# Values stationary, two query halves in two column tiles: turning the weighing of a float32 attention round

## What is computed

```python
h = rms_norm(x, g_pre) * (1 + scale) + shift
z = h @ w_in                     # q, k, v of A and B; q, k, v, gates of C; u
# A: 8 query heads, 2 kv heads, dim 64: softmax(q k^T / 8) @ v
# B: 4 heads, q and k in halves of 32, value dim 64
a = softmax(s1) - lam * softmax(s2);  o_b = rms_norm(a @ v, b_out_gain) * (1 - lam_init)
# C: bidirectional gated linear attention (GLA), then rms_norm per head
mixed = concat(o_a, o_b, o_c) * silu(u)
x_new = x + gate * rms_norm(mixed @ w_out, g_post)
```

## Time and profile before

| | before |
|---|---|
| median of three runs, us | 2540.59 |
| profiled execution: span, us | 2538.9 |
| profiled execution: own time beside the span | not recorded apart; the median lies 1.7 above the span |
| PE busy, share of the span | 2343.5, 92% |
| DVE, ACT, POOL busy, us | 1248.2, 874.2, 411.0 |
| attention of one layer, 563 to 1125 us: PE, DVE, ACT, POOL busy | 557.0, 267.2, 227.2, 82.9 of 562 |
| output block of one layer, 1125 to 1270 us: PE, DVE busy | 126.8, 80.4 of 145 |

### The profile page before, as it was taken

The page is one execution under the profiler, slowest core; times in us unless marked ns, Lnnn a source line. Parts: engine busy times, 40 slices in busy tenths (PEclk is TensorE's granted clock), DMA queues, the critical chain, the costliest instruction groups (busy, mean ns, idle before and its releaser), DMA issues. The chain is left out here.

```text
span 2538.9 us, 37284 instructions
## 1 busy us (share of the span) xinstructions
PE 2343.5 (92%) x14005; PEld 2004.6 (79%) x14005; DVE 1248.2 (49%) x2247; ACT 874.2 (34%) x1424; POOL 411.0 (16%) x344
## 2 busy tenths in 40 slices
PE   5799999879999999979958999998899999999798
PEld 3678987559999999977736789876599999999676
DVE  5667100865444454465466770008645444544554
ACT  5432211413444334442153322124143444344421
POOL 0211220420111111010002121114101111110200
PEclk9899999879999999989979999998799999999899
DMA  7332121010111111023273322210110111010232
GB/s 251 108 109 83 56 85 51 20 46 13 29 29 29 24 23 29 18 74 125 92 257 100 110 82 67 75 52 13 46 31 12 29 29 29 19 28 18 100 100 100
DMA packets 215017, 164.65 MB, mean 65 GB/s; under 512 B 162236, under 2 KB 164736, under 8 KB 214912
## 3 DMA queue, kind: packets, MB, share of 16 engines
q1 hardware_dynamic: 214912, 163.26, 21.4%
HBM read 124.80 MB, written 38.42 MB: 64 GB/s over the span
## 5 line engine op out<-in xcount | busy, mean ns | idle before, releaser
L1295 DVE TENSOR_REDUCE neg_max_parts<-work 128x1 f32<-128x512 f32 (+1 forms) x608 | 394.6, 687 | 410.6 <-PE work L1120 400.0
L1248 ACT ACTIVATE probs<-scores 128x1024 f32<-128x1024 f32 x320 | 327.7, 1025 | 566.7 <-PE scores L1138 338.1
L422 PE MATMUL z_acc<-w_hi,h_hi 128*128 128x512 f32 (+1 forms) x960 | 361.5, 377 | 12.4 <-DVE h_lo L539 7.6
L422 PE MATMUL z_acc<-w_hi,h_lo 128*128 128x512 f32 (+1 forms) x960 | 358.5, 373 | 0.0
L422 PE MATMUL z_acc<-w_lo,h_hi 128*128 128x512 f32 (+1 forms) x960 | 358.5, 373 | 0.0
L1159 PEld LDWEIGHTS att_out<-vB,probs 128*128 128x128 f32 x2688 | 336.4, 191 | 20.6 <-ACT probs L1248 7.7
L1159 PEld LDWEIGHTS att_out<-vA,probs 128*128 128x128 f32 x2688 | 339.3, 191 | 12.5
L1159 PE MATMUL att_out<-vB,probs 128*128 128x65 f32 x2688 | 336.2, 270 | 5.3 <-ACT probs L1248 4.8
L1159 PE MATMUL att_out<-vA,probs 128*128 128x65 f32 x2688 | 338.7, 270 | 0.0
L520 POOL TENSOR_TENSOR w_lo<-w_stage,w_hi 128x512 fp32r<-128x512 f32 (+1 forms) x112 | 134.7, 1231 | 824.1 <-ACT w_hi L455 824.1
L422 PEld LDWEIGHTS z_acc<-w_hi,h_hi 128*128 128x128 f32 x960 | 182.3, 190 | 47.4 <-DVE h_lo L539 9.2
(11 more groups left out here) (220 smaller groups left out, 3310.2 us busy)
## 6 DMA issues: line engine op xcount, KB each, us to landing
mod_w<-in_w_mod SPq DMA_DIRECT2D x24, 1024.0 KB, 7.6
w_stage<-in_w_in SPq DMA_DIRECT2D x96, 256.0 KB, 3.1
z_scratch<-z_out SPq DMA_DIRECT2D x60, 256.0 KB, 2.0
u_scratch<-z_out SPq DMA_DIRECT2D x40, 256.0 KB, 2.0
cv<-u_scratch SPq DMA_DIRECT2D x20, 512.0 KB, 5.8
out_y_sample<-y_tiles SPq DMA_DIRECT2D x16, 512.0 KB, 5.2
k_rawA<-z_scratch SPq DMA_DIRECT2D x16, 320.0 KB, 3.0
q_rawA<-z_scratch SPq DMA_DIRECT2D x16, 320.0 KB, 3.7
```

The lines of the kernel that those rows point to most:

```text
L422: mm = pe.matmul(acc, w_ap if w_first else h_ap, h_ap if w_first else w_ap, start=(k == 0 and q == 0), stop=(k == KD - 1 and q == 2))
L1248: act.activation(pr[:, b, :], sc[b][:, :, :].rearrange("p c n -> p (c n)"), ACT.Exp, scale=SCALE[u]).then_inc(s["a_exp"], 1)
L1295: dve.tensor_reduce(dst, src, AX_X, ALU.max, negate=True).then_inc(s["a_wkdve"], 1)
```

## The change

In the attention block the values become the stationary operand (64 columns) and the probabilities the moving one. The 1024 queries are two halves of 512; the first half's output stands on PSUM partitions 0 to 63, the second's on 64 to 127, so that they are two column tiles of the array. Outputs thus come transposed (head dimension on partitions) and stay so in `oa` and `ob`; the gate is made and stored transposed too, and the output block needs transposes for the GLA part alone. Row sums are no column of the values any more: GpSimd adds the probabilities of the key tiles (all but the last one in A, the last two in B) in `prob_sums`, and TensorE multiplies that sum and the left-out tiles by ones. The reciprocal is taken of 512 columns. `probs` has six buffers. The casts of the hi parts move from GpSimd to ScalarE. The steps stand in groups of two, the prompt is step 5 and no longer the last; all sixteen units are written out, without a loop. Two DMAs load B's gain by partition.

```diff
@@ attention: constants
-PREP_AT = (3, 3, 4, 4, 4, 3, 3, 3, 3, 0, 0)
-HALF = 5
+PROMPT_AT = 5
+TILE_AT = (0, 1, 2, 3, 4, None, 5, 6, 7, 8, 9)
+GROUPS = ((0, 1), (2, 3), (4, 5), (6, 7), (8, 9))
+NPB = 6
+DIRECT = {"A": 1, "B": 2}
@@ GpSimd
+            for p in range(UNITS):
+                u, h = of_unit(p)
+                for j in range(1, summed(p)):
+                    i = TILE_AT.index(j)
+                    n = p * STEPS + i
+                    pool.wait_ge(s["a_exp"], n + 1)
+                    a = acc[:, p % 2, :]
+                    if j == 1:
...
+                        ins = pool.tensor_tensor(a, pr[:, (n - 1) % NPB, :], pr[:, n % NPB, :], ALU.add)
+                    else:
+                        pool.wait_ge(s["a_add"], adds(p, i) - 1)
+                        ins = pool.tensor_tensor(a, a, pr[:, n % NPB, :], ALU.add)
+                    ins.then_inc(s["a_add"], 1)
+                    if j == 6 and p + 2 < UNITS:
+                        split_lo(pool, s, att, u, h + 1)
@@ TensorE
-                    mm = pe.matmul(o, probs, v[u][:, key, :], start=(j == 0 and t % HALF == 0),
-                                   stop=(j == KT_S - 1 or (j == KT_S and key == KT - 1)), skip_group_check=True)
+            def weigh(p, i):
...
+                pe.wait_ge(s["a_exp"], n + 1)
+                if i == 0:
+                    pe.wait_ge(s[f"a_v{u}"], 32 * (h + 1))
+                if i == 0 or i == PROMPT_AT:
+                    pe.wait_ge(s["a_out"], p + 1)
+                j = TILE_AT[i]
+                if j is not None:
+                    for rows, q in halves(NB):
+                        mm = pe.matmul(ob[rows, :], v[u][:, j, :], probs[:, q], start=(j == 0), stop=(j == KT_S - 1))
...
+            def sums(p):
+                u, h = of_unit(p)
+                pe.wait_ge(s["a_pout"], p + 1)
...
+                for x, src in enumerate(sources):
+                    if x == len(sources) - 1:
+                        pe.wait_ge(s["a_add"], adds(p, LAST))
+                    for rows, q in halves(NB):
+                        mm = pe.matmul(sm[rows, :], per["ones"][:, :], src[:, q], start=(x == 0), stop=(x == len(sources) - 1))
+                mm.then_inc(s["a_sum"], 1)
...
+            def run_unit(p):
+                nxt = p + 1
+                for g in range(len(GROUPS) - 1):
+                    pieces(nxt, 6 * g, 2)
+                    scores(p, GROUPS[g + 1][0])
+                    pieces(nxt, 6 * g + 2, 2)
+                    scores(p, GROUPS[g + 1][1])
+                    pieces(nxt, 6 * g + 4, 2)
+                    for i in GROUPS[g]:
+                        weigh(p, i)
+                pieces(nxt, 24, 2)
+                scores(p, LAST)
+                pieces(nxt, 26, 1)
+                for i in GROUPS[-1]:
+                    weigh(p, i)
+                pieces(nxt, PREP_LAST, PREP - PREP_LAST)
+                weigh(p, LAST)
+                sums(p)
+                if nxt < UNITS:
+                    for i in GROUPS[0]:
+                        scores(nxt, i)
@@ ScalarE, run_unit
+                for i in range(STEPS):
+                    exps(p, i)
+                    if nxt:
+                        if i in (1, 2, 3):
+                            for x in range(2 * i - 2, 2 * i):
+                                stand(nxt, x)
...
+                    if i == PROMPT_AT and p + 2 < UNITS:
+                        split_hi(u, h + 1)
@@ VectorE
+                    if p and i == 18:
+                        prompt_output(p - 1)
...
+            def prompt_output(p):
+                dve.wait_ge(s["a_pv"], p * STEPS + PROMPT_AT + 1)
+                dve.reciprocal(rsp[:, :], sm[:, P:2 * P]).then_inc(s["a_rs"], 1)
...
+            def output(p):
+                dve.wait_ge(s["a_sum"], p + 1)
+                dve.reciprocal(rs[:, :], sm[:, :]).then_inc(s["a_rs"], 1)
+                dve.wait_ge(s["a_rs"], 2 * p + 2)
+                weighted(p, ob, rs, 0, NB).then_inc(s["a_out"], 1)
...
-                do(dve.tensor_tensor(csq[:, :, :], oc[:, :, :], oc[:, :, :], ALU.mult))
+                for t in range(0, T, 2):
+                    do(dve.tensor_tensor(csq[:, :, :], oc[:, t:t + 2, :], oc[:, t:t + 2, :], ALU.mult))
...
@@ projection
-            if kind in ("z", "u"):
+            if kind == "z":
                 uses += [(b, kind, t) for t in range(T)]
+            elif kind == "u":
+                uses += [(b, f"u{m}", tb) for m in range(NB // P) for tb in range(3)]
@@ output block
-                dve.tensor_reduce(bst[:, t % 2, 0, :], bsq[:, :, :], AX_X, ALU.add).then_inc(s["o_bss"], 1)
+                do(dve.tensor_tensor(bd[:, t % 2, :, :], o[:, 0, :, tile_rows(t)], o[:, 1, :, tile_rows(t)], ALU.add))
+                dve.tensor_tensor(bsq[:, :, :], bd[:, t % 2, :, :], bd[:, t % 2, :, :], ALU.mult).then_inc(s["o_bsq"], 1)
...
+                do(dve.reciprocal(bst[:, b, :, :], bst[:, b, :, :]))
...
+                pe.matmul(bs[t % 2][:, :, :].rearrange("p k t -> p (k t)"), per["pair_ones"][:, :],
+                          bsq[:, :, :].rearrange("p k t -> p (k t)"), start=True, stop=True).then_inc(s["o_bss"], 1)
...
             turn(0)
+            turn(1)
+            turn(2)
```

More of the change, by code:

```diff
@@ L193, in _ @@
                 sp.dma_start(per["gains"][:, i, :], layer(io[name]).broadcast_to([P, HEAD_DIM])).then_inc(s["m_small"], 16)
+            for r in range(2):
+                sp.dma_start(per["b_gain"][r * B_V:(r + 1) * B_V, :], layer(io["b_out_gain"]).rearrange("a d -> d a")).then_inc(s["m_small"], 16)
             sp.dma_start(lam_c[:, :], layer(io["lam_consts"]).broadcast_to([P, 2])).then_inc(s["m_small"], 16)
@@ L398, in _ @@
                         store_z(b, t)
-                    elif kind == "u":
-                        store_u(b, t)
-            n = Z_BLOCKS * T + 2 * T
+                if kind == "u":
+                    for i in range(first_use[b], last_use[b] + 1):
+                        store_u(i)
+            n = Z_BLOCKS * T + len([u for u in uses if u[1][0] == "u"])
             for i in range(3):
@@ L1045, in attention_block, with of_unit, summed, adds @@
         m_cols = {A: qst2[:, :, HEAD_DIM:HEAD_DIM + 2], B: qst[B][:, :, 3 * B_QK:KR[B]]}
[L1046 to L1052, removed]
-            return 2 * h + (0 if u == A else 1)
+        def of_unit(p):
+            return "AB"[p % 2], p // 2
+        def summed(p):
+            return KT_S - DIRECT["AB"[p % 2]]
+        def adds(p, i):
+            before = sum(summed(x) - 1 for x in range(p))
+            j = len([t for t in TILE_AT[:i + 1] if t is not None and t < summed(p)])
+            return before + max(j - 1, 1)
+        def halves(t):
+            return [(slice(c * HEAD_DIM, (c + 1) * HEAD_DIM), slice(c * t, (c + 1) * t)) for c in range(2)]
         @block.sync
@@ new lines, in weigh @@
+            def weigh(p, i):
+                u, h = of_unit(p)
+                n = p * STEPS + i
+                probs = pr[:, n % NPB, :]
+                pe.wait_ge(s["a_exp"], n + 1)
+                if i == 0:
+                    pe.wait_ge(s[f"a_v{u}"], 32 * (h + 1))
+                if i == 0 or i == PROMPT_AT:
+                    pe.wait_ge(s["a_out"], p + 1)
+                j = TILE_AT[i]
+                if j is not None:
+                    for rows, q in halves(NB):
+                        mm = pe.matmul(ob[rows, :], v[u][:, j, :], probs[:, q], start=(j == 0), stop=(j == KT_S - 1))
+                else:
+                    for what in range(2):
+                        for c in range(2):
+                            for rows, q in halves(P):
+                                lhs = per["ones"][:, :] if what else v[u][:, KT_S + c, :]
+                                mm = pe.matmul(sm[rows, what * P:(what + 1) * P], lhs, probs[:, c * NB + q.start:c * NB + q.stop],
+                                               start=(c == 0), stop=(c == 1))
+                mm.then_inc(s["a_pv"], 1)
@@ new lines, in pieces @@
+            def pieces(p, first, n):
+                if p < UNITS:
+                    for i in range(first, first + n):
+                        prep(p, i)
+            def run_unit(p):
[19 more added lines that the diff above has]
+                        scores(nxt, i)
@@ new lines, in split_hi @@
+            def split_hi(u, h):
+                w = QK_W[u]
+                k, q, ks, qs = att["kraw"][u], att["qraw"][u], kst[u], qst[u]
+                act.wait_ge(s[f"a_raw{u}"], 48 * (h + 1))
+                if u == A:
+                    act.copy(ks[:, :, 0:w], k[:, :, :])
+                    act.copy(qs[:, :, w:2 * w], q[:, :, :])
+                else:
+                    for x in range(2):
+                        act.copy(ks[:, :, x * w:(x + 1) * w], k[:, :, :])
+                    act.copy(qs[:, :, 2 * w:3 * w], q[:, :, :])
+                act.copy(qs[:, :, 0:w], q[:, :, :]).then_inc(s[f"a_hi{u}"], 1)
```

384 lines of the change are left out of this document (176 added, 208 removed).

## The result

The changed kernel takes 2577.94 us (median, 2577.3 to 2578.28) against 2540.72 for the kernel before: ratio 1.0144, 95% interval 1.013 to 1.0159. It is 37 us slower; the forecast was 2529, 12 faster.

The account below looks back on a forecast made before the run. TensorE was taken as the bound, its weighing records paced by loads of the probabilities. Loop -12.6, first unit -4.4 and last unit +11 gave -6 a layer, -12 for two: 2540.6 - 12 = 2529 us, range 2455 to 2610.

Parts of the forecast that it names:

- rival (d): Attention loop: TensorE's clock spends 20 us a turn at half, +10 a pair, 2680 in total; chance 0.04.
- the first group of B: Start of a B unit, where pieces wait for ScalarE's casts between exponentials: 8.3 us against 5.3 dense.
- The pair's walk: Attention loop, step by step: A 33.2 plus B 36.3 make 69.5 us against 71.3, -12.6 a layer.
- the signs that the prediction named: Trace marks of a right forecast, such as a pair of 66 to 73 and B's cast waits of some 3 us.
- Column tiles: Weighing: products of the two 64-column tiles run together, so a key tile costs 0.86 us instead of 1.72.
- change of shape: TensorE's array form between pieces and weighings: a round trip costs 0.31 us, six a unit, 1.6.
- reciprocal: VectorE's reciprocal of the row sums, now 512 columns: 3.5 us, with two products 5.0 instead of 1.04.
- rival (c): Weighing: the column tiles run one after another for 512 columns, 2780 in total; chance 0.04.
- The first unit: First attention unit of a layer, from the last scores before it: 32.3 us instead of 36.7, -4.4 a layer.
- The last unit: Last attention unit, squares held by GpSimd's adds and output bare: 36.6 us against 25.7, +11 a layer.
- The output block: Output stage after attention, with fewer transposes and other VectorE work: together -3 to +4 us a layer.
- Rival (b): Unit ends: GpSimd's adds hold VectorE's small steps, 2 to 4 us a unit, 2600; with added handshakes chance 0.30.

Follow-up runs that it names:

- e1_fill: Changed kernel with four score products made twice more in the first group of every B unit but the last, filling TensorE's waits; 2552.47 us.
- e8: Changed kernel with each group's two weighings set apart between the pieces, from the second group on; 2594.11 us, ratio to before 1.0203.
- e5: Changed kernel with 16 of the 21 maxima in a unit reading only the first 256 columns of each bank; 2540.38 us, single run.
- e4: Changed kernel with GpSimd adding only the first pair of key tiles of each unit, so row sums lack tiles; 2561.56 us, single run.
- e2: Changed kernel with ScalarE's second casts of A's key pieces replaced by one later copy from SBUF; 2533.69 us, ratio to before 0.9967.
- e13: Changed kernel with both products of the first query half before both of the second, in four of five groups; 2577.66 us, single run.

## Why the prediction was wrong

**The step that failed** is rival (d), "The clock falls", at a chance of 0.04, and with it the first group of B, costed at the full clock though the text itself gave it "4.9 in 8.3". e1_fill gives the pair without falls: 34.65 + 35.9 = 70.55. The changed kernel's mean is 73.2; 2.65 x 14 = 37 us, the whole of the loss. The page of before showed the fall after a stretch with no more idle time than this one (2.07 us there, in 3.33 of 5.40; 2.13 here, in 4.75 of 6.88). It was priced as all or nothing (20 us at half clock a turn); what came was 3.4 to 10.2 a turn, in every turn.

**The pair's walk** was good. A's groups, forecast and measured (cut behind the next unit's first scores, so their sums are 33.8 in A and 36.8 in B): first 6.35 and 6.38; middle 5.48 and 5.6; with the prompt 6.9 and 6.8; end 9.0 and 9.4. B, without falls: 8.3 and 8.23; 5.43 and 5.47; 6.9 and 6.7; end 10.3 and 10.9. The sum of 69.5 was 1.05 short, mostly in the sums and small handshakes of the end: 15 us over fourteen pairs. Without the falls the kernel would stand near 2541 (an estimate, 2578 less 37), no change, so even then the gain would not have come. Of the signs that the prediction named, the pair of 73.2 lies just outside the 66 to 73 of a right one; the waits for the casts were 2.1 us, not 3.

**Column tiles, change of shape, reciprocal.** Eight records fill 1.94 (two lines of four, last one's own end included), a round trip costs 0.35 (the first record 0.20 late behind a piece, the next piece 0.15 behind 1.72 of records), the reciprocal of 512 columns 3.36 against 3.5. All three stand; rival (c) is out. (Its price was also too high by its own terms: half of 11.2 to 12.1 is 6 a unit and not 8, which gives 2720 and not 2780.)

**The first unit** gave -2.1 to -2.3 a layer, not -4.4. From its first scores to its reciprocal it takes 3.0 and 3.8 less; the rest (0.9 and 1.6) is lost in the stages ahead of it, which the sum had at nothing and no run takes apart. The clock is lower in it too, 0.55 in its first 5.7 us (561.0 to 566.7), 0.80 in the same window before.

**The last unit** gave +9.7 (forecast +11) by the named steps: squares of 2.0 between adds, ScalarE held 5.7 us, a bare output of 5. Its fall of 6.8 us, which the forecast did not have, cost little behind these: the adds end last even so. **The output block** gave -1 to -3, inside -3 to +4.

**The books**: 2529 + 37 (falls) + 15 (walk) + 4 (first units) - 3 (last) - 4 (output) = 2578, as measured.

**Rival (b)** had the right mechanism for a neighbouring kernel: e8 and e5 show it, and that the margin was one add, as it said. In this one it costs some 0.13 an A unit (e4).

## What to carry to other kernels

Taking work off TensorE, whose clock fell here behind stretches with too much idle time, can cost more than the work was worth. When a walk through the new order leaves waits on TensorE that the old one did not have, price the stretch behind each at both clock levels, and look for such a fall in the old trace for how full the engine was before it. Then shorten the wait, or fill it: here 0.46 us of repeated products in each B unit's wait bought 14 us.

## What the runs showed of the hardware that was not expected

- The granted clock depends on more than the work of the last microseconds: two B units of e2 with 4.87 of 5.76 and 4.89 of 5.78 us of work went different ways.
- No single wait is long where it falls: in the first groups of all fourteen B units the longest is 1.12 us, and three waits leave 2.13 of 6.88 us idle.
- Products of two column tiles run side by side although two of one tile stand ahead of two of the other in the program (e13: 1.94 for eight records in both orders). The Trainium skill (TensorEngine Tiling (Array Packing), Key Properties) has tiles operate independently; the trace agrees.
- GpSimd holds off VectorE's copy with a single SBUF input too: 128x10 in 0.18 without the adds (e4), 0.62 beside them in most A units of the changed kernel, 2.13 in e8. The Trainium skill (SBUF — State Buffer, "SBUF: two separate sides") says that a VectorE instruction in a 2-port mode takes the lock too, and that a float32 copy from SBUF to SBUF runs in one. By that rule, the trace agrees.
- A reciprocal costs VectorE 0.96 us for 128 columns, 1.75 for 256 and 3.36 for 512, the last five times a maximum over 512 (0.69).
